# First turns of the expert retrieval in another order, first places of the ring in another order, and four more slots per pass on VectorE

## The reference, cut to what matters

```python
q = (xc @ wq).reshape(c, PEER_HEADS, 2, PEER_QDIM // 2)
sc = jnp.einsum('thpd,hpkd->thpk', q, keys)
top_v, top_i = lax.top_k(sc, PEER_TOPK)                  # 16 of 128 keys, twice for each of 8 heads
cand = (top_v[:, :, 0, :, None] + top_v[:, :, 1, None, :]).reshape(c, PEER_HEADS, -1)
best_v, best_pos = lax.top_k(cand, PEER_TOPK)            # 16 of 256 pairs
ids = jnp.take_along_axis(cand_id, best_pos, axis=-1)
gate = jax.nn.softmax(best_v, axis=-1)
act = jax.nn.gelu(jnp.einsum('td,thkd->thk', xc, u_tab[ids])) * gate
return jnp.einsum('thk,thkd->td', act, v_tab[ids])
```

## Time and profile before

| | before |
|---|---|
| median of three runs | 1573.01 us |
| profiled execution | 1573.96 us, its span 1572.2 us |
| TensorE matmul busy | 1375.0 us, 87% |
| VectorE busy | 1155.2 us, 73% |
| ScalarE, GpSimd busy | 454.9 us, 605.7 us |
| bytes moved | 627.87 MB, mean 399 GB/s |
| of these by the gathers | 537.97 MB, 83.0% of the DMA engines' span |
| chain that ended last | PE 45%, DMA 30%, DVE 15%, issue 6% |

### The profile page before, as it was taken

The page is one execution under the profiler, slowest core; times in us unless marked ns, Lnnn a source line. Parts: engine busy times, 40 slices in busy tenths (PEclk is TensorE's granted clock), DMA queues, the critical chain, the costliest instruction groups (busy, mean ns, idle before and its releaser), DMA issues.

```text
span 1572.2 us, 15089 instructions
## 1 busy us (share of the span) xinstructions
PE 1375.0 (87%) x4622; PEld 747.1 (48%) x4622; DVE 1155.2 (73%) x2745; ACT 454.9 (29%) x1096; POOL 605.7 (39%) x525
## 2 busy tenths in 40 slices
PE   8899999999696997988888699999879787877877
PEld 4668445654473443544365245555437433333333
DVE  6929989787688886874668887886658987665555
ACT  3523244343211233342122134343112222121112
POOL 1003345444243334553434334544443443333332
PEclk9989999999798998998999899999989899899899
DMA  9548999999999999999999999999999999999998
GB/s 355 224 147 343 422 421 421 405 417 421 423 402 422 422 402 405 422 420 422 421 418 419 420 415 417 421 394 383 421 423 421 410 406 421 421 422 420 423 420 341
DMA packets 89820, 627.87 MB, mean 399 GB/s; under 512 B 10081, under 2 KB 11361, under 8 KB 20750
## 3 DMA queue, kind: packets, MB, share of 16 engines
q0 software_dynamic: 74144, 537.97, 83.0%
q1 hardware_dynamic: 15598, 88.95, 14.0%
HBM read 625.82 MB, written 1.06 MB: 399 GB/s over the span
## 4 chain that ended last, share of the span: by engine, by line
PE 45%; DMA 30%; DVE 15%; issue 6%; ACT 3%; POOL 1%; SPq 0%; DVEq 0%; ACTq 0%
DMA ring<-table_uv,ids 29%; PE ps L1765 25%; DVE ring L1360 6%; PE ps L1729 5%; PE ps L1529 3%; PE ps L1480 2%; PE ps L1696 2%; PE ps L1519 1%; ACT diag L868 1%; ACT acts L843 1%; PE ps L1596 1%; POOL ring L1829 1%; PE ps L1781 1%; PE ps L1606 1%; DVE weights L1369 1%
## 5 line engine op out<-in xcount | busy, mean ns | idle before, releaser
L1765 PE MATMUL ps<-ring,diag 128*128 128x512 f32 x1884 | 893.8, 630 | 173.7 <-ACT diag L868 169.9
L1829 POOL DMA_INDIRECT ring<-table_uv,ids x512 | 600.0, 1172 | 931.9 <-PE ps L1765 776.9
L1765 PEld LDWEIGHTS ps<-ring,diag 128*128 128x128 f32 x1884 | 372.0, 202 | 644.8 <-issue 636.1
L1360 DVE CUSTOM_DVE_ANT_0 ring<-ring,h 128x1024 f32<-128x1024 f32 x384 | 456.0, 1223 | 150.9 <-DMA ring<-table_uv,ids 148.0
L843 ACT ACTIVATE acts<-dots,small 128x4 f32<-128x4 f32 x126 | 37.5, 297 | 883.0 <-DVE dots L1360 856.6
L1360 DVE CUSTOM_DVE_ANT_0 ring<-ring,ps 128x1024 f32<-128x1024 f32 x120 | 144.6, 1220 | 98.9 <-DMA ring<-table_uv,ids 98.6
L868 ACT ACTIVATE diag<-cst,weights 128x128 f32<-128x128 f32 x471 | 151.4, 390 | 29.1 <-DVE weights L1369 28.9
L1729 PEld LDWEIGHTS ps<-hT,W 128*128 128x128 f32 x896 | 101.9, 192 | 3.5 <-issue 2.9
L1729 PE MATMUL ps<-hT,W 128*128 128x128 f32 x896 | 103.0, 275 | 0.2 <-ACT hT L710 0.2
L1529 PE MATMUL ps<-W,hT 128*128 128x512 f32 (+2 forms) x160 | 60.1, 529 | 1.3 <-DVE hT L991 1.3
L1696 PE MATMUL ps<-W,hT 128*128 128x512 f32 x128 | 57.3, 593 | 0.8 <-DVE hT L1205 0.8
(11 more groups left out here) (322 smaller groups left out, 1217.4 us busy)
## 6 DMA issues: line engine op xcount, KB each, us to landing
W<-peer_wq SPq DMA_DIRECT2D x9, 2048.0 KB, 13.0
W<-w_out SPq DMA_DIRECT2D x6, 2048.0 KB, 13.2
W<-w_in SPq DMA_DIRECT2D x8, 1282.0 KB, 10.9
ring<-table_uv,ids POOLq DMA_INDIRECT x512, 13.1
W<-w_in SPq DMA_DIRECT2D x8, 898.0 KB, 10.5
W<-peer_wq SPq DMA_DIRECT2D x12, 512.0 KB, 12.9
W<-w_in SPq DMA_DIRECT2D x8, 768.0 KB, 9.4
W<-w_in SPq DMA_DIRECT2D x8, 514.0 KB, 12.1
```

Of the source, the lines that this page charges most:

```text
L1360: v.tensor_tensor_reduce(ring_u[:, r, :], ring_u[:, r, :], tokens, 1.0, 0.0, ALU.mult, ALU.add, dots[:, s:s + 1]).then_inc(dots_done, 1)
L1765: mm = pe.matmul(ps[:, c, :], diag[:, s, :], ring_v[:, r, c * 512:(c + 1) * 512], start=(k == 0), stop=(k == SLOTS - 1), skip_group_check= ...
L1829: gp.indirect_dma_start(ring[:, place(t), :], None, table_uv, bass.IndirectOffsetOnAxis(ap=ids[:, b, k:k + 1], axis=0)).then_inc(pair_in[p ...
```

## The change

It does four things. In the first turns of pass 0, query 1 comes ahead of query 5; the rows of v of turns 0 and 1 come ahead of queries 2 and 3; dots come ahead of the search (best, pairs, ids) of their turn; the copy of queries 2 and 3 on ScalarE is a step of its own ("queried") behind the weigh of the next turn. The projections of pass 1 come in turns 3 to 5 instead of 2 to 5, and ids 2 in turn 6 instead of 5. The first eight requests use eight places, the next four use places that earlier slots free, and places 0 and 1, which hold the weights of query 2, come in as requests 12 and 13. Turns 5, 13, 15 and 16 of the first three passes join those whose fourth slot is on VectorE.

```diff
--- before.py
+++ after.py
@@ -36,11 +36,13 @@
 RING_G = 4
 HELD = 2 * RING_G
 RING = 10
-PLACES = (7, 2, 3, 4, 5, 6, 8, 9, 0, 1)
+FIRST_PLACES = (7, 2, 3, 4, 5, 6, 8, 9)
+PLACES = (7, 2, 3, 4, 0, 1, 5, 6, 8, 9)
+FRESH = (4, 5)
 PASSES = DEPTH * NB
 HALVES = SLOTS // RING_G
 SINGLE = HALVES * PASSES - 2
-ADD_FIRST, ADD_LAST = 20, 30
+ADDED = (5, 13, 15, 16, *range(20, 31))
 
 
 
@@ -157,7 +159,7 @@
               ["query 0", "mean 1"]]
     search = [["score 0", "query 1", "best 0"], ["score 1", "query 2", "best 1"], ["score 2", "pairs 0"],
               ["query 3", "ids 0"], ["score 3", "best 2"], ["best 3"]]
-    spread = [["pairs 1"], [], ["ids 1"], [], ["pairs 2"], [], [], ["ids 2"], [], [], ["pairs 3"], [], [], ["ids 3"]]
+    spread = [[], ["pairs 1"], [], ["ids 1"], ["pairs 2"], [], [], ["ids 2"], [], [], ["pairs 3"], [], [], ["ids 3"]]
     tail = [["pairs 1"], ["ids 1"], ["pairs 2"], ["ids 2"], ["pairs 3"], ["ids 3"]]
     mix = start + middle + search
     assert len(mix) <= HALVES
@@ -188,15 +190,13 @@
              ["glu", "mixed rows 0"],
              ["out 0", "gated", "mixed rows 1", "out 1", "out 2", "out 3"],
              ["rows 1", "square 1", "gain", "query 4", "mean 1", "score 4"],
-             ["quick 0", "next columns 3", "next columns 4", "next columns 5", "next columns 6", "next columns 7", "next z", "best 4", "pairs 4", "query 5", "score 5", "ids 4", "best 5", "query 1", "score 1"]]
+             ["quick 0", "next columns 3", "next columns 4", "next columns 5", "next columns 6", "next columns 7", "next z", "best 4", "pairs 4", "ids 4", "query 1", "query 5", "score 5", "score 1"]]
     for names in first:
         do(names, 0)
 
 
-    inner = [["best 1"], ["rows 0", "best 2"], ["project 0", "best 3"],
-             ["project 1", "project 2", "project 3", "pairs 1", "ids 1"],
-             ["project 4", "project 5", "pairs 2"],
-             ["row", "project 6", "project 7", "ids 2", "z"]]
+    inner = [[], ["best 1"], ["best 2"], ["rows 0", "project 0", "pairs 1", "ids 1"], ["project 1", "project 2", "project 3", "best 3"],
+             ["row", "project 4", "project 5", "project 6", "project 7", "pairs 2", "z"], ["ids 2"]]
     behind = {15: ["pairs 10"], 16: ["pairs 11"], 17: ["ids 10"], 18: ["ids 11"]}
     late = {18: ["steps 1", "phases 1"], 19: ["angles 0"], 20: ["angles 1", "angles 2"], 21: ["angles 3", "angles 4"],
             22: ["sines 1"], 23: ["tables 1"]}
@@ -204,7 +204,7 @@
     for n in range(PASSES):
         if n == 0:
             own = [[name for name in names if name.split()[0] in ("best", "pairs", "ids")] for names in inner]
-            mixing = [[name for name in names if name.split()[0] not in ("best", "pairs", "ids")] for names in inner] + middle + search
+            mixing = [[name for name in names if name.split()[0] not in ("best", "pairs", "ids")] for names in inner[:-1]] + middle + search
         else:
             own = tail if n + 1 < PASSES else spread
             mixing = mix if n + 1 < PASSES else []
@@ -220,26 +220,26 @@
             plan.append(("weigh", n, i))
             if i == 0 and n:
                 plan.append(("gathered", n - 1, 0))
+            if n == 0 and i in (1, 2):
+                do([f"queried {i + 1}", f"score {i + 1}"], n)
+            if i == 0 or n == 0 and i == 1:
+                plan.append(("rows of v", n, i))
+            if n == 0 and i < 2:
+                do([f"query {i + 2}"], n)
             if n == 0 and i == 0:
-                do(["pairs 5", "ids 5", "query 2"], n)
-            if n == 0 and i == 1:
-                do(["query 3"], n)
-            if i == 0:
-                plan.append(("rows of v", n, i))
-            if n == 0 and i == 0:
-                do(["score 2"], n)
+                do(["best 5", "pairs 5", "ids 5"], n)
+            if n == 0 and i == 3:
+                do(mixing[i], n + 1)
             if i < len(own):
                 do(own[i], n)
-            if i < len(mixing):
+            if i < len(mixing) and (n or i != 3):
                 do(mixing[i], n + 1)
             if n == 0:
                 do(behind.get(i, []), n)
             if n < NB:
                 do((late, later)[n].get(i, []), n)
-            if i:
+            if i > 1 or n and i:
                 plan.append(("rows of v", n, i))
-            if n == 0 and i == 1:
-                do(["score 3"], n)
     plan.append(("gathered", PASSES - 1, 0))
     return plan
 
@@ -462,15 +462,18 @@
 
         def place(t):
 
-            return PLACES[t % RING]
+            return FIRST_PLACES[t] if t < len(FIRST_PLACES) else PLACES[(t - len(FIRST_PLACES)) % RING]
 
         def before(t):
 
-            return t - RING if t >= RING else None
+            u = t - len(FIRST_PLACES)
+            if u < 0 or u in FRESH:
+                return None
+            return t - RING if u > max(FRESH) else u
 
         def filled(t):
 
-            return t // RING + 1
+            return 1 if before(t) is None else filled(before(t)) + 1
 
         def found_ids(n, i):
 
@@ -478,7 +481,7 @@
 
         def added(m):
 
-            return m // HALVES < PASSES - 1 and ADD_FIRST <= m % HALVES <= ADD_LAST
+            return m // HALVES < PASSES - 1 and m % HALVES in ADDED
 
         adds_by = [0]
         for m in range(HALVES * PASSES):
@@ -808,15 +811,19 @@
                 a.activation(hT[:, k:k + 2, :], by(ps[:, 5, i * 256:i * 256 + 256], P), ACT.Copy).then_inc(mT_act, 1)
 
             def query(n, i):
+                if n or i not in (2, 3):
+                    queried(n, i)
+
+            def queried(n, i):
                 if i == 4:
                     a.wait_ge(head_q_ps, 1)
                     a.activation(queries(n, 0)[:, 0], by(ps[:, 6, 0:256], P), ACT.Copy).then_inc(head_qT, 1)
                     return
                 if i == 5:
-                    a.wait_ge(qT_ps, 1)
+                    a.wait_ge(qT_ps, 2)
                     a.activation(queries(n, 0)[:, 1], by(ps[:, 6, 256:512], P), ACT.Copy).then_inc(qT_ready, 1)
                     return
-                a.wait_ge(qT_ps, 4 * n + i + 1)
+                a.wait_ge(qT_ps, 1 if (n, i) == (0, 1) else 4 * n + i + 1)
                 a.activation(queries(n, i % 2), ps[:, 6 + i % 2, :].rearrange("p (a c t) -> p a c t", a=2, t=P), ACT.Copy).then_inc(qT_ready, 1)
 
             def find_ids(n, i):
@@ -871,7 +878,7 @@
                   "next square": next_square, "next mean": next_mean, "next rows": next_rows, "next z": next_z,
                   "row": layer_row, "z": z_out, "s5 in": s5_inputs, "keys": keys, "qk sums": qk_sums, "softmax": softmax,
                   "weights": head_weights, "co sums": co_sums, "s5 out": s5_output, "gate rows": gate_rows, "glu": glu_out,
-                  "mixed rows": mixed_rows, "query": query, "ids": find_ids, "h out": h_out, "dots": take_dots, "weigh": weigh, "dot": take_dot, "weigh one": weigh_one})
+                  "mixed rows": mixed_rows, "query": query, "queried": queried, "ids": find_ids, "h out": h_out, "dots": take_dots, "weigh": weigh, "dot": take_dot, "weigh one": weigh_one})
 
         @block.vector
         def _(v):
@@ -1707,7 +1714,7 @@
                     if n:
                         pe.wait_ge(rows_act, 4 * (2 * n + 2))
                 elif q >= 2:
-                    pe.wait_ge(qT_ready, 4 * n + q - 1)
+                    pe.wait_ge(qT_ready, 4 * n + q - 1 if n else 2)
                 later = n - n // 3
                 if q == 0:
                     pe.wait_ge(wq_first_in, 16 * (n // NB + 1))
@@ -1741,7 +1748,7 @@
                 if part[-1] == 1:
                     pe.wait_ge(head_qT, 1)
                 else:
-                    pe.wait_ge(qT_ready, 4 * n + q + 1)
+                    pe.wait_ge(qT_ready, 4 * n + q + 1 if n or q else 2)
                 bank = 5 if part[0] == 2 else 2 + q
                 if (n, q) == (0, 3):
                     pe.wait_ge(sc_used, searched(0, 5))
@@ -1824,8 +1831,10 @@
                             gp.wait_ge(z_ps, 4)
                         elif t == 3:
                             gp.wait_ge(z_ps, 8)
-                        elif t in (6, 8):
-                            gp.wait_ge(qT_ps, t // 2 - 1)
+                        elif t == 6:
+                            gp.wait_ge(qT_ps, 1)
+                        elif t == 12:
+                            gp.wait_ge(qT_ps, 3)
                         gp.indirect_dma_start(ring[:, place(t), :], None, table_uv,
                                               bass.IndirectOffsetOnAxis(ap=ids[:, b, k:k + 1], axis=0)).then_inc(pair_in[place(t)], 16)
 
```

## The result

The changed kernel took 1587.12 us (median of 4 runs, 1582.76 to 1591.12) against 1573.01: a ratio of 1.0091, 95% interval 1.0068 to 1.0114. Run again beside the last experiments it was 1.0117 (1.0095 to 1.0140). The forecast was 1585 in a range of 1570 to 1592, slower. Nothing of the change lies ahead of it. TensorE had only 3.4 us at half clock there instead of the 17 us of the kernel before. Across the 14 profiles here the first request starts between 109.35 and 118.17. **So I compare marks after subtracting the first request's start.** Read so, the changed kernel is 8.7 + 7.1 = 15.8 us longer in its profile.

The account below looks back on a forecast made before the run. Up to 302 us a compute chain with nearly no slack was taken as the bound, with the DMA stream leading afterwards. Profiled 1573.96 + 12.7 (chain delay) - 1.5 (slots) = 1585.2, given as 1585, range 1570 to 1592.

Parts of the forecast that it names:

- requests 6 and 8: First turns: these requests go out near 128.5 and 136.8 us, filling two early DMA holes, about 4.5 us of stream.
- wait for chunk 7: Turn 5: chunk 7's load waits for chunk 4's use at 206.2, lands at 216.1, so TensorE waits from 212.2.
- weigh 7 late: VectorE, turn 7: weigh 7 ends at 240.6 us against 227.86, 12.7 us late.
- The main step: Turns 8 to 14 win nothing back, so the chain's 12.7 us delay at 302 us carries to the end.
- Rival A: Whole kernel: the DMA stream leads throughout and covers the late projections, giving 1567 to 1570 us; chance 0.12.
- ids 2 behind z_out: VectorE, before weigh 7: this search step, formerly ahead of z_out, now follows it and adds 5.4 us.
- The hole at chunk 7: DMA stream, from about 216 us: late rows 5 leave GpSimd nothing to request, a hole of 7.5 us.
- the slots: Places 5, 13, 15, 16 in three passes: TensorE matmul pairs become VectorE adds; bounds +2 to -5, taken as -1.5 us.
- Places 15 and 16 shorten turns where TensorE leads: Turns 15 and 16: moving the fourth slot to VectorE, adds of 1.285 for matmul pairs of 6.87/4 = 1.72, shortens them.
- half of the dips in pass 2: DMA stream dips, such as 6 us lacking from 1022 to 1100 us: regaining half of them bounds the gain at -5.
- Place 5 of pass 0 lies in VectorE's wait for the projection: nothing either way: Turn 5 of pass 0: the added VectorE add falls in idle time, costing and gaining nothing.
- Rival C: TensorE after pauses of 2.6 and some 4 us: half clock costs 3.5 to 7.5 more, 1588 to 1593 us; chance 0.15.

Follow-up runs that it names:

- e12: The changed kernel itself, run again on the chip of the last experiments: ratio 1.0117 (1.0095 to 1.0140) to the kernel before.
- e11: The changed kernel without its added slots, second run, on the same chip as e9, e10 and e12: ratio 1.0075 (1.0056 to 1.0095) to the kernel before.
- e1: The changed kernel without its added slots, only turns 20 to 30 keeping the fourth slot on VectorE, first run: 1.0081 (1.0054 to 1.0109).
- e5: Kernel before with query 1 ahead of query 5, dots 0 ahead of best 5, rows 0 ahead of query 2, new places: 0.9997 (0.9983 to 1.0012).
- e8: The changed kernel without added slots and with ids 2 back in turn 5 ahead of z_out: 1.0058 (1.0043 to 1.0074).
- e9: e5 with the change's projections in turns 3 to 5, ids 2 ahead of z_out: 1.0031 (1.0014 to 1.0048).
- e10: e9 with rows of v of turn 1 ahead of query 3 besides: 1.0060 (1.0042 to 1.0078).
- e7: Kernel before with only places 13, 15 and 16 added to the slots on VectorE: 1.0016 (1.0000 to 1.0031).
- e6: Kernel before with only place 5 added to the slots on VectorE: 1.0026 (1.0011 to 1.0041).
- e2: Kernel before with only the slots changed, places 5, 13, 15 and 16 of three passes added on VectorE: 1.0055 (1.0034 to 1.0075).

## Why the prediction was right, step by step

Times are behind the first request; before it stood at 116.47.

| step | forecast | changed kernel |
|---|---|---|
| requests 6 and 8 | 12.0, 20.3 | 12.0, 19.9 |
| TensorE's wait ahead of score 2 | 2.6 | 1.86; 1.86 in e12, then half clock |
| first chunk load | 49.8 | 48.5 |
| VectorE's wait for the transposes | 6 | 5.6 |
| wait for chunk 7 | 3.9 | 2.0; 3.5 in e12, then half clock |
| last projection ends | 102.6 | 100.3 |
| hole in the stream | 7.5 us | 6.6, then 3.9 |
| weigh 7 late | 12.7 | 10.0; 15.9 in e12; 13.0 in e11, without slots |

The main step, that a delay of the compute chain at turn 14 is a delay of the end, held in every order that was run: weigh 14 and the last turns are late by the same, within 2 us, wherever no slots are added (e1, e5, e8, e9, e10, e11). Rival A, the stream whose lead covers the late projections, fell with the changed kernel itself: the stream ran dry at 207.5 us. e5 doesn't bear on it, since its stream won a net 1.6 us only. Of the terms inside the delay, ids 2 behind z_out was sized right (5.4). The hole at chunk 7 was right in place and kind.

**The term that was mis-sized is the slots:** -1.5 forecast, +8.6 by themselves and +6.6 on top of the order. The step that failed is "Places 15 and 16 shorten turns where TensorE leads", and with it the half of the dips in pass 2 that was to come back. I priced the adds by TensorE's work that goes. In these turns TensorE waits for VectorE's diagonals: 7.6 us between 290 and 350 us in e7 and in both profiles of the change, 2.8 before, 1.6 in e11. So the add is paid, and the longer waits were followed by half clock. "Place 5 of pass 0 lies in VectorE's wait for the projection: nothing either way" held in the changed order, within 0.3 us. It fails only in the order of before, where e6 and e2 tested it and VectorE has no such wait.

Rival C, the clock, was part of what happened, and of the order's delay too, not only of the slots': rows 7 took 9.71 with and without added slots. The sum had nothing for it. The text ahead gives 0.51 over 15 us for the clock after 74.95; the row shown under it is of 5 us only, at 0.52.

So the errors partly cancel. In the first profile, where rows 7 are the only piece at half clock between the first request and turn 14, weigh 7 is 10.0 late and not 12.7: the chain was forecast too long. In e11 and e12 the clock brings it to 13.0 and 15.9. The order alone costs 12 to 13 us by the ratios, as forecast, in part for a reason that the sum left out. With the slots' true price the sum would have been 1593 to 1595, beyond the whole range and nearer to the second run's +18 than to the first median. That 1585 lay so near 1587 is in part luck.

What stays open: how the slots' loss divides between adds paid on VectorE and lost clock. No kernel was run that keeps the clock up with the adds in place, and none that fills the early holes for good, which would show what the stream alone can win. And no version beat the kernel before: e5, the best, has 0.9997 (0.9983 to 1.0012).

## What to carry to other kernels

A DMA stream that is busy in every slice can still be fed by a chain without slack. Ask when its queue runs dry (here at 306 us before, at 207.5 after), and price a reordering by what it does to that chain's last common point. Count a filled hole only net of those that open behind it: e5 filled 3.5 us and kept 1.6. When work is moved later on an engine, look at what then waits first in that engine's line: here a load chained to chunk 4, a copy that stood ahead of a search, and 5.4 us of search that slid from an idle stretch into the chain. Work taken from an engine that already waits is no gain, and here its clock fell besides. And take a second profile of a kernel before naming a cause for 5 us: two profiles of the change differed by that much.

## What the runs showed of the hardware that was not expected

The stage ahead of the first request, which is the same in all kernels here, took 109.4 to 118.2 us in 14 profiles, and it moved with the time at half clock in it: 109.35 with 3.4 us, 113.70 with 13.7, 118.17 with 23.9. The two profiles of the changed kernel differ by 4.4 us there, 0.3% of the execution.

The same wait of TensorE was not always followed by the same clock. Behind 1.86 us ahead of score 2 the next two pieces took 8.2 us in one profile of the change and 9.9 in the other, and in e1 and e11. Behind waits for chunk 7 of 2.03, 2.75, 3.46 and 3.98 us its projection took 3.28, 4.80, 6.10 and 5.88. And a wait that grew from 1.62 to 5.19 us was followed by a stretch at half clock in which four rows took 9.48 us instead of 7.10.
